# Expert weights: four pieces of the next expert are loaded ahead into 32 KB of their own and copied into place for each unit

## What is computed

```python
def expert_block(args):
    xe, e = args
    gu = xe @ w_gate_up[e] + b_gate_up[e]
    gate = jnp.minimum(gu[:, :D_FF], SWIGLU_LIMIT)
    up = jnp.clip(gu[:, D_FF:], -SWIGLU_LIMIT, SWIGLU_LIMIT)
    act = (up + 1.0) * gate * jax.nn.sigmoid(SWIGLU_ALPHA * gate)
    return act @ w_down[e] + b_down[e]
```

## Time and profile before

| | |
|---|---|
| median of three runs | 3032.16 us (3027.61 to 3032.35) |
| profiled execution, span | 3025.3 us (its own time is not listed apart) |
| PE busy | 2841.0 us, 94% of the span |
| VectorE busy | 1377.2 us, 46% |
| ScalarE, GpSimd busy | 846.3 us, 303.8 us |
| HBM read | 593.89 MB |
| chain that ended last | PE 79%, DMA 10% |
| loads of expert weights | 384 of 1024 KB, median 11.4 us from issue to landing |

### The profile page before, as it was taken

How to read it: one execution, slowest core, us unless ns; L and a number is a source line. 1 busy time by engine, 2 the same in 40 slices (tenths; PEclk the granted TensorE clock), 3 DMA queues, 4 the chain that set the end, 5 groups by cost and what they waited for, 6 DMA issues and landing times.

```text
span 3025.3 us, 41220 instructions
## 1 busy us (share of the span) xinstructions
PE 2841.0 (94%) x15088; PEld 1753.1 (58%) x15089; DVE 1377.2 (46%) x2323; ACT 846.3 (28%) x1661; POOL 303.8 (10%) x291
## 2 busy tenths in 40 slices
PE   8999999999999978888989898879999999999999
PEld 5665656746888422222323232226877888888887
DVE  5768678644455211112112121124674786555551
ACT  4547365501212211111211121113243544211100
POOL 0101011310001000000000000003111553000000
PEclk9999999999999988999989998989999999999999
DMA  5433425355124899979798989997120222122111
GB/s 226 160 112 132 150 95 205 154 199 194 67 89 166 337 410 405 409 316 402 313 404 348 387 328 410 411 411 290 56 115 17 92 81 98 35 89 86 61 65 60
DMA packets 137826, 634.03 MB, mean 210 GB/s; under 512 B 12848, under 2 KB 55728, under 8 KB 77040
## 3 DMA queue, kind: packets, MB, share of 16 engines
q1 hardware_dynamic: 110832, 562.65, 47.3%
q0 software_dynamic: 10112, 35.66, 3.6%
q10 hardware_dynamic: 16768, 34.17, 3.1%
HBM read 593.89 MB, written 36.44 MB: 208 GB/s over the span
## 4 chain that ended last, share of the span: by engine, by line
PE 79%; DMA 10%; DVE 4%; ACT 3%; issue 2%; POOL 1%; SPq 0%; ACTq 0%; DVEq 0%; POOLq 0%
PE ps L340 27%; PE ps L2767 17%; PE ps L2747 9%; PE ps L2317 9%; DMA slot<-in_w_exp 8%; PE ps L279 3%; PE ps L2464 2%; DMA w_modT<-in_w_modT 2%; PE ps L3030 2%; PE ps L2473 2%; PE ps L3002 1%; PE ps L2738 1%; PE ps L2985 1%; PE ps L2256 1%; ACT decay L1818 1%
## 5 line engine op out<-in xcount | busy, mean ns | idle before, releaser
L2767 PE MATMUL ps<-slot,xT_blk 128*32 128x512 f32 (+1 forms) x3328 | 615.7, 638 | 137.7 <-DMA slot<-in_w_exp 137.3
L2767 PEld LDWEIGHTS ps<-slot,xT_blk 128*32 128x32 f32 (+1 forms) x3328 | 159.3, 128 | 497.3 <-issue 307.5
L2747 PE MATMUL ps<-slot,aT 128*32 128x256 f32 (+1 forms) x2528 | 286.5, 454 | 0.0
L3729 DVE MEMSET b_there<- 128x1 f32 x52 | 3.1, 59 | 494.7 <-DMA b_few<-in_b_gu 482.2
L2747 PEld LDWEIGHTS ps<-slot,aT 128*32 128x32 f32 (+1 forms) x2528 | 111.3, 119 | 183.8 <-issue 152.4
L3733 DVE TENSOR_TENSOR gate<-ps,b_row 128x256 f32<-128x256 f32 (+1 forms) x52 | 29.0, 558 | 344.1 <-PE ps L2767 344.1
L340 PE MATMUL ps<-in_t,in_s 128*128 128x264 f32 x528 | 124.8, 387 | 0.5 <-issue 0.5
L2464 PE MATMUL ps<-hT,slot 128*128 128x512 f32 x256 | 120.7, 604 | 2.2 <-ACT zT L1763 2.1
L2317 PE MATMUL ps<-h_sum,w_sum 128*128 128x384 f32 (+1 forms) x384 | 120.2, 460 | 0.0
L1980 ACT ACTIVATE y_row<-ps 128x512 f32<-128x512 f32 (+1 forms) x52 | 25.5, 490 | 333.2 <-PE ps L2747 333.2
L340 PEld LDWEIGHTS ps<-in_t,in_s 128*128 128x128 f32 x528 | 100.5, 190 | 17.8 <-DVE in_s L429 0.9
(11 more groups left out here) (572 smaller groups left out, 4984.9 us busy)
## 6 DMA issues: line engine op xcount, KB each, us to landing
slot<-in_w_exp SPq DMA_DIRECT2D x384, 1024.0 KB, 11.4
in_w<-in_w_ffn SPq DMA_DIRECT2D x22, 1024.0 KB, 4.8
expert_rows<-zero SPq DMA_DIRECT2D x4, 4608.0 KB, 24.3
slot<-in_w_xbc SPq DMA_DIRECT2D x8, 2048.0 KB, 8.2
sum_here<-sum_rows ACTq DMA_DIRECT2D x32, 512.0 KB, 3.7
w_modT<-in_w_modT POOLq DMA_DIRECT2D x32, 512.0 KB, 3.9
rnn_w<-in_w_rnn SPq DMA_DIRECT2D x16, 1024.0 KB, 4.9
out_w<-in_w_ffn_out SPq DMA_DIRECT2D x8, 1408.0 KB, 7.5
```

Of the source, the lines that this page charges most:

```text
L2747: last = pe.matmul(ps[j * rows:(j + 1) * rows, Y_BANK_OF[s], 0:width], aT[s][:, 2 * half + c, tile * rows:(tile + 1) * rows], slot[4 + k / ...
L2767: last = pe.matmul(GATE_PS[s][tile * rows:(tile + 1) * rows, half, :], xT_blk[:, k, first:first + rows], slot[piece // 4][:, at:at + 512], ...
```

## The change

A second area of 32 KB per partition, "ahead", holds four gate/up loads (4 to 7) of the next expert. The slots where these loads went until now are called "held", and `span` is one tensor over both areas and what lies between. SP now loads pieces 4 to 7 of expert q+1 into the area ahead, once the first unit of expert q has had its copies. Before every unit but the first, four copies of 128x2048 f32 bring pieces 4 to 7 into place: from the area ahead if the unit begins a new expert, and onto themselves if it does not (`held_from` is the offset, 0 or TO_AHEAD). VectorE does them behind "act" of the unit before: all four for a 64-row unit, three for a 32-row one, for which GpSimd does the first (`copy_4`) once PE has done piece 9 of the unit before. PE waits for the copy of a piece instead of its load. The last expert is taken out of SP's loop, since nothing follows it. Several buffers move to make room (`up`, `sig`, `b_row`, `meta_x`, `last_y` and others), and the recurrence of the second block waits for loads on other semaphores.

```diff
+AHEAD = 4
...
         def load_piece(i, e):
-            sp.dma_start(slot[i // 2][:, i % 2 * 2 * PIECE:(i % 2 + 1) * 2 * PIECE], row(io["w_exp"], e * LOADS + i)).then_inc(exp_loaded[i], 16)
+            there = GU_LOADS - AHEAD <= i < GU_LOADS
+            sp.dma_start(held(i - (GU_LOADS - AHEAD)) if there else slot[i // 2][:, i % 2 * 2 * PIECE:(i % 2 + 1) * 2 * PIECE], row(io["w_exp"], e * LOADS + i)).then_inc(exp_loaded[i], 16)
...
-        with sp.Fori(1, NE) as q:
-            u = sp.value_load(first_unit[0:1, bass.ds(q, 1)], min_val=1, max_val=UNITS)
-            e = sp.value_load(expert_at[0:1, bass.ds(q, 1)], min_val=0, max_val=NE - 1)
-            for i in range(GU_LOADS):
+        def load_ahead(i, e):
+            sp.dma_start(held(i - (GU_LOADS - AHEAD), TO_AHEAD), row(io["w_exp"], e * LOADS + i)).then_inc(exp_loaded[i], 16)
+
+        def load_gate_up(e, u):
+            for i in range(GU_LOADS - AHEAD):
                 sp.wait_ge(moe_gu.sem, moe_gu.before(f"gu{2 * i + 1}", u))
                 load_piece(i, e)
             sp.wait_ge(moe_dve.sem, moe_dve.before("spread", u))
             load_bias(e)
+
+        def load_down(e, u):
             for i in range(DN_PIECES // 2):
                 sp.wait_ge(moe_dn.sem, moe_dn.before(f"dn{2 * i + 1}", u + 1))
                 load_piece(GU_LOADS + i, e)
 
+        e_first = sp.value_load(expert_at[0:1, 1:2], min_val=0, max_val=NE - 1)
+        moe_gu.after(sp, "gu0")
+        for i in range(GU_LOADS - AHEAD, GU_LOADS):
+            load_ahead(i, e_first)
+        with sp.Fori(1, NE - 1) as q:
...
+            load_gate_up(e, u)
+            sp.wait_ge(moe_copy4.sem, moe_copy4.before("copy4", u))
+            load_ahead(4, e_next)
+            for i in range(5, GU_LOADS):
+                sp.wait_ge(moe_copies.sem, moe_copies.before(f"copy{i}", u))
+                load_ahead(i, e_next)
+            load_down(e, u)
...
-                        if piece % 2 == 0:
+                        if piece % 2 == 0 and piece < 2 * (GU_LOADS - AHEAD):
                             pe.wait_ge(exp_loaded[piece // 2], e * 16 + (exp_first[piece // 2] + 16))
+                        elif piece == 8:
+                            pe.wait_ge(moe_copy4.sem, moe_copy4.before("copy4", u))
+                        elif piece % 2 == 0:
+                            pe.wait_ge(moe_copies.sem, moe_copies.before(f"copy{piece // 2}", u))
...
                 moe_dve.done(dve.tensor_tensor(gate[s][:], gate[s][:], sig[s][:], ALU.mult), "act")
+                if more:
+                    for k in range(s, AHEAD):
+                        dve.wait_ge(exp_loaded[4 + k], e_next * 16 + (exp_first[4 + k] + 16))
+                        copied = dve.tensor_copy(held(k), span[:, bass.ds(from_at + k * 2 * PIECE, 2 * PIECE)])
...
+        def copy_4(i):
+            u = 2 * i + 2
+            e = pool.value_load(expert_of[0:1, bass.ds(u + 1, 1)], min_val=0, max_val=NE - 1)
+            from_at = pool.value_load(held_from[0:1, bass.ds(u, 1)], min_val=0, max_val=TO_AHEAD)
+            pool.wait_ge(moe_gu.sem, moe_gu.at("gu9", u - 1))
+            pool.wait_ge(exp_loaded[4], e * 16 + (exp_first[4] + 16))
+            moe_copy4.done(pool.tensor_copy(held(0), span[:, bass.ds(from_at, 2 * PIECE)]), "copy4")
...
             pool.tensor_copy(token_now[:], token_u[:, bass.ds(i + 2, 1)]).then_inc(s_now, 1)
+            copy_4(i)
             pool.wait_ge(moe_xT_pe.sem, moe_xT_pe.at("half1", i))
```

More of the change, by code:

```diff
@@ L1067, in program @@
     gate = [area(f"gate{s}", [P, s + 1, PART]) for s in range(2)]
[L1068 to L1069 removed]
     aT = [area(f"aT{s}", [P, 2 * (s + 1), P]) for s in range(2)]
+    meta_x = area("meta_x", [P, KD, N_META])
+    square_meta = area("square_meta", [P, KD, N_META])
+    b_there = area("b_there", [P, 1])
+    AHEAD_AT = END // 32 * 32 - AHEAD * SLOT_BYTES // 2
+    assert area.next <= AHEAD_AT
+    area = Area(AHEAD_AT)
+    area.next += AHEAD * SLOT_BYTES // 2
+    assert area.next <= END
+    HELD_AT = FREE + (GU_LOADS - AHEAD) * SLOT_BYTES // 2
+    span = at("span", [P, (END // 32 * 32 - HELD_AT) // 4], HELD_AT)
+    TO_AHEAD = (AHEAD_AT - HELD_AT) // 4
     area = Area(AFTER_TABLES, AFTER_H)
     b_few = [area(f"b_few{s}", [P, s + 1, 2 * PART]) for s in range(2)]
[L1073 to L1076, removed]
+    exp_loaded = w_loaded + [sem(f"exp_loaded{i}") for i in range(6, 16)]
+    exp_first = loads + [0] * 10
     TURN_AT, DOWN_AT = [8, 4], [10, 6]
@@ L1093, in program, with held @@
     AT_BANK, Y_BANK_OF = [3, 5], [7, 6]
+    def held(k, at=0):
+        return span[:, at + k * 2 * PIECE:at + (k + 1) * 2 * PIECE]
     s_gate_zero = sem("s_gate_zero")
@@ L2767, in gate_up @@
                             last = pe.matmul(GATE_PS[s][tile * rows:(tile + 1) * rows, half, :], xT_blk[:, k, first:first + rows],
-                                             slot[piece // 4][:, at:at + 512], start=(k == 0), stop=(k == KD - 1))
+                                             weights[:, at:at + 512], start=(k == 0), stop=(k == KD - 1))
                         moe_gu.done(last, f"gu{piece}")
@@ L3730, in turn @@
                 moe_dve.done(dve.stream_shuffle(b_row[s][:], b_few[s][:], [0] * 32), "spread")
+                more = not (s and last)
+                if more:
+                    e_next = dve.value_load(expert_of[0:1, bass.ds(u + 2, 1)], min_val=0, max_val=NE - 1)
+                    from_at = dve.value_load(held_from[0:1, bass.ds(u + 1, 1)], min_val=0, max_val=TO_AHEAD)
                 dve.wait_ge(moe_dve.sem, moe_dve.at("spread", u))
@@ L3744, in turn @@
                 moe_dve.done(dve.tensor_tensor(gate[s][:], gate[s][:], sig[s][:], ALU.mult), "act")
+                if more:
+                    for k in range(s, AHEAD):
+                        dve.wait_ge(exp_loaded[4 + k], e_next * 16 + (exp_first[4 + k] + 16))
+                        copied = dve.tensor_copy(held(k), span[:, bass.ds(from_at + k * 2 * PIECE, 2 * PIECE)])
+                        if k == 0:
+                            moe_copy4.done(copied, "copy4")
+                        else:
+                            moe_copies.done(copied, f"copy{4 + k}")
         with dve.Fori(0, i_last) as i:
@@ L4116, in _ @@
             gather(token_now[:])
+        copy_4(i_last - 1)
         pool.wait_ge(s_yrow[0], n * Y_STORES[0])
```

43 lines of the change are left out of this document (33 added, 10 removed).

## The result

The changed kernel takes 3075.4 us (median of four, 3068.6 to 3076.0); the kernel before, on the same chip, 3029.9 us. That is 45.5 us more, a ratio of 1.0151 (95% interval 1.0134 to 1.0167). The profiled execution took 3075.89 us with a span of 3074.1 us, 48.8 us more than the span before.

The account below looks back on a forecast made before the run. Loads of expert weights were taken to limit the expert stage most of the time, PE in the dips. Longer expert transitions plus the start sum to 58.6 us, say +59: 3032.2+59 = 3091, range 3062 to 3118.

Parts of the forecast that it names:

- a faster kernel: The buffer fills the DMA dips of the expert stage: -41 us and a few more, some 2987; 9%.
- no change: Only the order of loads changes and DMA stays as busy as now: 3032; 4%.
- F to F: Between successive experts' first-unit gate/up ends (F): 67 to 70 us behind two- and three-unit experts; 64 or less is wrong.
- The slow case: Copies at one element per cycle (+12), or lower PE clock after longer waits: +75 to +95, 3107 to 3127; 17%.
- two units, 64 then 32 rows: Transitions behind experts 1, 4, 8, 24, 28: 68.6 us each, 18.3 us added in all.
- two units, 32 then 64: Transitions behind experts 6, 16, 26: 69.1 us each, 15.0 us added in all.
- experts 10+11, 13+14: Pairs of a three-unit and a two-unit expert: 121.4 us per pair, 10.9 us added in all.
- experts 18+19, 21+22: Pairs of a two-unit and a three-unit expert: 118.6 us per pair, 11.4 us added in all.
- start: Stage start: B(1) (gate/up loads 4 to 7) goes out ahead of A(1) (loads 0 to 3): 3 us added.
- end: Stage end: no B behind the last expert; C(31), its down loads, lands within time PE needs anyway: 0.
- E to F: Last unit's gate/up end (E) to next expert's F: 53.2 us behind 32-row units, 50.4 behind 64-row.
- The step on the order: Load order A(q), B(q), bias, C(q) becomes A(q), bias, B(q+1), C(q): A(q) comes four loads (10 us) later.

Follow-up runs that it names:

- early copies: VectorE makes copies 4 to 6 once the unit has read these pieces, copy 7 still behind "act", against the changed kernel: 3033.2 us, ratio 1.0017.
- the first of the two kernels: Changed kernel with GpSimd making copy 4 for every unit, the gather behind its second copy: 3072.0 us, ratio 1.0134.

## Why the prediction was right, and where it was off

**Sign and size.** +45.5 us against a forecast of +59; 3075.4 lies inside 3062 to 3118. The rivals of a faster kernel and of no change fell: the dips stayed, and F to F from a two-unit expert is 66.0 to 69.4 us (three of eight below the 67 to 70 that were forecast), nowhere 64 or less. The slow case fell too: a copy takes 1.22 us, and though the granted clock of the stage is 0.91 instead of 0.92, F comes 20.5 to 22.4 us after load 0 of A, in the twelve loops, as before (20.6 and 21.8). One reading of the slices was incomplete: the 28th, in which the stage ends, is at 290, below the 313 that the prediction calls the lowest; nothing hangs on it.

**The terms of the sum.**

| term | predicted | measured |
|---|---|---|
| two units, 64 then 32 rows (five) | 18.3 | 12.2 |
| two units, 32 then 64 rows (three) | 15.0 | 15.7 |
| experts 10+11, 13+14 | 10.9 | 9.0 |
| experts 18+19, 21+22 | 11.4 | 10.0 |
| one-unit experts | 0 | -1.2 |
| start | 3 | 7.3 |
| end | 0 | -5.7 |
| sum | 58.6 | 47.3 |

The span grew by 48.8 us, of which 1.5 lie behind the stage. E to F behind a 64-row unit was put at 50.4 and is 50.2. Behind a 32-row unit it was put at 53.2 and is 52.0 in the mean (50.5 to 53.3). The gate makes most of that: the first load ahead goes out at E + 3.8, where the terms gave 4.55, for the 0.55 us of reading a table do not stand between "act" and the copy, and from the copy to SP it takes 0.2 us instead of 0.3. The second part is the way from the first load ahead to load 0 of A. I took 22.6 us with the gather in it, and this holds for six of seven (22.2 to 23.3); but expert 30's first unit has 32 rows, no gather falls in, and it is 20.2. The term of 21.3 us from load 0 to F was right (21.2 in the mean); it holds the 12.5 to 14.8 us behind A's last load, and most of the scatter.

**Start and end were mis-sized, in opposite directions.** Of the start's 7.3 us, 3.0 are there at F(0) already, ahead of any effect of the loads; over the fourteen profiles of this study F(0) lies anywhere from 1003.9 to 1011.3. The rest, 4.3, is B(1) ahead of A(1), as foreseen. At the end F(31) comes 53.0 us later than before, but the last load lands only 47.3 us later (2116.9 against 2069.6), and the program goes on from that load: GpSimd's first gather waits for it, before and after.

```profile
2069.83 0.97 POOL L4131 DMA_INDIRECT picked_rows<-expert_rows,y_row_u  x1 [30.94 <-DMA slot<-in_w_exp]
```

```profile
2117.15 1.01 POOL L4210 DMA_INDIRECT picked_rows<-expert_rows,y_row_u  x1 [25.07 <-DMA slot<-in_w_exp]
```

The prediction gave the end 0, as C(31) had been waited for there before. It did not see that C(31) then had B(31) in front of it, which now has long landed. In both kernels C(31) begins to be issued 11 us before F(31); its last load took 16.1 us to land before and takes 10.2 now. In the table the start lies 4.3 us over its forecast and the end 5.7 under; that they nearly cancel is luck.

**The step on the order was incomplete.** "What it costs is what PE still has to do after the needed load", says the prediction, and adds the gate behind "act" as a second part of the loop. The arithmetic of the loop was right, but not the weight of the parts. The kernel before had E to F of 49.0 and 45.1 us, and F to F there was near the pace of the stream (24 loads at 31.65 us per twelve are 63.3 us). Only what goes over these two numbers shows. The changed kernel is 3.0 us over seven times and 5.1 us over five times: 46.5 us. With early copies it is 0.9 and 0.4 over, F(3) to F(31) is 1.3 us longer, and the 4.3 us that remain are the start's 9 (F(0) to F(3) is 90.2 us against 81.0) less what the end gives back (F(31) to GpSimd's first gather is 1.7 us there, 7.8 before). So the late gate is what the change pays for in the middle of the stage, and the order of loads only makes the loop long enough for the gate to matter: with two pieces instead of four, and gates that are at most 2.3 us earlier behind a 32-row unit, the cost is a tenth.

**What was costed at nothing.** PE never waits for a copied piece (0.0 in the group above), as forecast. GpSimd's copy takes 1.89 us, inside 1.3 to 4.0, and hides. The moved buffers cost nothing, by a run of their own. PE's wait for loads was put at 190 us and is 186.9. The gathers do not meet VectorE's copies: they take 1.07 us each to issue, 1.06 before. The Trainium skill (VectorE: DVE Perf Modes, "Mode 2×_2P") gives two elements per cycle for such a copy. From 64 to 2048 columns the copies grow by 0.52 ns per column ((1219 - 190) / 1984): by that rule, the trace agrees, as this is half of the 1.05 ns that two-input rows take.

## What to carry to other kernels

A buffer that runs ahead helps only if it lets a load go earlier than before; read which instruction frees it, and what that stands behind. A copy that frees a buffer belongs behind the last reader of its piece, not behind the engine's longest chain, but nothing as long as itself may stand ahead of an activation for which the tensor engine waits. In an in-order queue every load is as late as the latest gate in front of it, so a gate is priced by the longest loop that runs through it, and slack against the stream's own pace comes off first.

## What the hardware showed that was not expected

GpSimd's and VectorE's copies exclude each other. In the changed kernel they never meet, and each of the 179 on VectorE takes 1.22 us. With GpSimd copying for every unit, 18 of GpSimd's 51 copies meet two of VectorE's each. The one that is under way when GpSimd's begins keeps its 1.22 us. The one that starts 0.07 us after GpSimd's takes 2.91 to 2.92 us, and each of these 18 ends 1.08 us after GpSimd's. The timeline of VectorE and then of GpSimd, in the first of the two kernels that do this:

```profile
1217.15 5.18 DVE L3807 COPY span<-span 128x2048 f32 x3
```

```profile
1219.35 1.90 POOL L4180 COPY span<-span 128x2048 f32 x1 [8.94 <-PE ps L2816]
1221.22 1.17 POOL L4191 TENSOR_TENSOR token_there<-cst 128x1 f32<-128x1 f32 x1
```

Three copies take 5.18 us where three without GpSimd's take 3.49. The one that starts at about 1219.4 lasts 2.92 us, while GpSimd's keeps its 1.90. GpSimd's tiny operation behind it then takes 1.17 us instead of 0.19. The Trainium skill (SBUF — State Buffer, "SBUF: two separate sides") says that the two engines share a pair of ports as an exclusive lock, which one holds for the whole instruction while the other stands still: by that rule, the trace agrees. What the collisions cost here was not tried by itself; the two kernels that have them are not slower than the changed one. A gather that meets a copy of VectorE's takes longer too. With the down loads first, six gathers start up to 0.2 us ahead of such a copy and take 1.38 to 1.54 us to issue, the eighteen others 1.06 to 1.08.
